# Rounded three-pass input projections in the second layer of a two-block transformer kernel

## The reference, cut to what matters

```python
hx = adaln(x, norm1_g[layer], mod_x[0], mod_x[1]); hc = adaln(ctx, ...)
qa_x, ka_x, va_x, qm_x, km_x, vm_x, om_x, gt_x = split_columns(hx @ w_in)
qa_c, ka_c, va_c, qm_c, km_c, vm_c, om_c, gt_c = split_columns(hc @ w_in)
att_x = window_attention(q, k, v, k_ctx, v_ctx, sink_g)          # 8 heads, softmax with a sink
h_xf, h_xb = mlstm_chunkwise(conv(qm), conv(km), vm, gates ...)  # forward and backward memory
out_x = merge_groups(att_x, h_xf + flip(h_xb), om_x, ...)        # @ w_out
```

## Time and profile before

| | us |
|---|---|
| median of 3 runs (lowest, highest) | 2455.31 (2447.01, 2457.3) |
| profiled execution | 2452.7 |
| its span | 2450.9 |
| TensorE busy | 2379.6 (97%) |
| DVE busy | 1808.3 (74%) |
| ACT busy | 1306.2 (53%) |
| GpSimd busy | 86.3 (4%) |

### The profile page before, as it was taken

One profiled execution on the slowest core, in us unless ns is written; L12 is line 12 of the kernel. 1 busy time (PEld: TensorE's weight loads), 2 busy tenths in 40 slices (PEclk: granted clock), 3 DMA queues, 4 the chain that ended last, 5 costly groups with the idle time before them and its releaser, 6 DMA issues.

```text
span 2450.9 us, 33383 instructions
## 1 busy us (share of the span) xinstructions
PE 2379.6 (97%) x13253; PEld 1953.4 (80%) x13253; DVE 1808.3 (74%) x2855; ACT 1306.2 (53%) x1971; POOL 86.3 (4%) x89
## 2 busy tenths in 40 slices
PE   7999899999999998999999999999999999999998
PEld 2575558788777776888888888888798999989997
DVE  6764577677553545999999999999867776677774
ACT  3245332222233444877877778777744654546554
POOL 0000010000010000000000000000000001100002
PEclk8999999999999999999999999999999999999999
DMA  7411045555432114989889889898843455434552
GB/s 296 180 61 35 1 154 192 190 204 188 151 138 86 52 35 173 361 329 356 343 329 366 332 329 367 331 367 331 314 173 121 155 181 198 166 127 145 182 190 103
DMA packets 71651, 510.68 MB, mean 208 GB/s; under 512 B 7905, under 2 KB 9057, under 8 KB 10049
## 3 DMA queue, kind: packets, MB, share of 16 engines
q1 hardware_dynamic: 68690, 500.21, 54.8%
q10 hardware_dynamic: 2208, 6.32, 0.7%
q0 software_dynamic: 592, 1.97, 0.2%
HBM read 506.23 MB, written 2.23 MB: 207 GB/s over the span
## 4 chain that ended last, share of the span: by engine, by line
PE 88%; DVE 7%; ACT 4%; issue 1%; DMA 1%; ACTq 0%; DVEq 0%
PE bank L815 86%; DVE UL L2238 2%; ACT UH L1703 1%; PE bank L1273 1%; DMA consts<-in_c 1%; PE bank L952 1%; DVE arena L2246 1%; DVE HT L2238 0%; ACT L1706 0%; DVE arena L3026 0%; ACT arena L1706 0%; DVE arena L2238 0%; ACT arena L1949 0%; DVE arena L2242 0%; DVE small L2305 0%
## 5 line engine op out<-in xcount | busy, mean ns | idle before, releaser
L2238 DVE TENSOR_TENSOR UL<-ring,UH 128x1024 fp32r<-128x1024 f32 (+1 forms) x804 | 975.1, 1220 | 313.2 <-ACT UH L1703 293.3
L1703 ACT CAST UH<-ring 128x1024 fp32r<-128x1024 f32 (+1 forms) x804 | 834.8, 1041 | 572.2 <-PE bank L815 543.0
L815 PE MATMUL bank<-XH,UH 128*128 128x256 f32 x1040 | 298.4, 288 | 11.3 <-ACT XH L1706 8.2
L815 PE MATMUL bank<-UH,HGh 128*128 128x512 f32 (+1 forms) x768 | 291.3, 379 | 3.9 <-issue 2.8
L815 PE MATMUL bank<-XH,UL 128*128 128x256 f32 x1040 | 294.1, 284 | 0.0
L815 PE MATMUL bank<-XL,UH 128*128 128x256 f32 x1040 | 288.9, 284 | 0.0
L815 PE MATMUL bank<-UH,HGl 128*128 128x512 f32 (+1 forms) x768 | 288.3, 375 | 0.0
L815 PE MATMUL bank<-UL,HGh 128*128 128x512 f32 (+1 forms) x768 | 287.4, 374 | 0.0
L2285 DVE CUSTOM_DVE_ANT_0 JUNK<-ring,CROW 128x1024 bf16<-128x1024 f32 x176 | 210.2, 1237 | 15.6 <-ACT CROW L1706 9.6
L815 PEld LDWEIGHTS bank<-XH,UH 128*128 128x128 f32 x1040 | 200.6, 193 | 14.7 <-issue 10.3
L815 PEld LDWEIGHTS bank<-XH,UL 128*128 128x128 f32 x1040 | 200.6, 193 | 0.0
(11 more groups left out here) (231 smaller groups left out, 3940.5 us busy)
## 6 DMA issues: line engine op xcount, KB each, us to landing
ring<-in_w SPq DMA_DIRECT2D x477, 1024.0 KB, 4.8
XT<-in_x ACTq DMA_DIRECT2D x2, 1024.0 KB, 11.8
bias_scratch<-BIAS POOLq DMA_DIRECT2D x6, 192.0 KB, 2.1
consts<-in_c ACTq DMA_DIRECT2D x1, 1109.0 KB, 8.1
out_y<-XT ACTq DMA_DIRECT2D x2, 512.0 KB, 3.5
BIAS<-bias_scratch POOLq DMA_DIRECT2D x1, 768.0 KB, 6.8
constd<-in_c ACTq DMA_DIRECT2D x1, 768.0 KB, 4.2
consts<-in_c ACTq DMA_DIRECT2D x1, 512.0 KB, 17.3
```

What stands on the lines that cost most here:

```text
L815: return e.matmul(out, lhsT, rhs, start=start, stop=stop, skip_group_check=True)
L1703: return e.copy(out, in_)
L2238: return e.tensor_tensor(out, a, b, op)
```

## The change

The input projections of layer 1 go over to the second way, with three float32r products.

- `conv_in` is removed. cp2 and cp3 run as a `duo` (one unit each, input blocks in the outer loop, the data's low parts two blocks late), then cp0, cp1, q0 to q3 and kf as `split` steps of one unit each.
- Values and gates are regrouped. One pass over 272 columns (attention values 128, gates 16, the memory values of head 0, 128) in three units of 3, 3 and 2 input blocks; one pass over 384 columns (heads 1 to 3) in four units of 2 blocks, 768 columns each. All four token blocks are worked on within each unit.
- om becomes eight units of 512 columns.
- The low parts of the four 384-column units and of the eight om units are made on GpSimd, one at the place of the step in its program; its `since` clear moves from the `mxz` step to `emt_mm`.
- Low parts overwrite the ring slot in place, so a slot comes free only when the products of its units are done. High parts lie in two thirds of the fourth ring slot and in a free buffer, so this stage has three ring slots. (The ring returns to four in the expert stage.)
- The data's high parts (`HHM`) are made by ACT behind each affine pass, their low parts (`HL`) by DVE over `H`.
- Three units are cast ahead of the root. In the split and value steps the look-ahead is one unit (`UNITS - 1`).
- `BESIDE[1]` becomes (1, 3, 3, 3) behind the four 384-column steps and (1, 2, 1, 2, 1, 2, 1, 2) behind om.

```diff
-          {"vm": (0, 1, 1, 1, 1, 2, 2, 2), "om": (1, 2, 1, 2, 1, 1, 1, 2)})
+          {"vm": (1, 3, 3, 3), "om": (1, 2, 1, 2, 1, 2, 1, 2)})
...
-            out.append(("conv_in", l, [((("cp", l, j), k), "w_in", (l,), [(128 * k, 768 + 128 * j, 128)])
-                                       for j in range(4) for k in range(8)]))
-            for j in range(4):
+            duo(("cp", l, 2), ("cp", l, 3), "w_in", (l,), 1024, 1152)
+            out.append(("evict", ("cp", l, 2)))
+            out.append(("evict", ("cp", l, 3)))
+            for j in range(2):
+                split("cp", l, j, key="w_in", idx=(l,), c0=768 + 128 * j)
                 out.append(("evict", ("cp", l, j)))
...
+            for ks in ((0, 1, 2), (3, 4, 5), (6, 7)):
+                name = ("vg", l, 0, ks[0])
+                out.append(("rows1", l, 0, ks, [(name, "w_in", (l,), [(128 * k, c, n) for k in ks
+                                                                      for c, n in ((640, 128), (2304, 16), (1280, 128))])]))
...
+        for j in range(4 * l):
+            ks = (2 * j, 2 * j + 1)
+            name = ("vg", l, 1, ks[0])
+            out.append(("rows1", l, 1, ks, [(name, "w_in", (l,), [(128 * k, 1408, 384) for k in ks])]))
+            if j == 0:
+                for _ in range(6):
+                    more()
+            beside("vm", j)
...
+        def by_pool(u):
+            name = W.units[u]
+            return W.stage_of[u] == "mixed" and (name[0] == "vg" and name[2] == 1 or name[0][0] == "om")
...
+            if stage == "mixed":
+                n, off, _ = W.at[piece]
+                o = W.place[n] * SLOT + off
+                return u, (YSlt[:, 512:512 + w], ring_[:, 3 * SLOT:3 * SLOT + w], ring_[:, 3 * SLOT + UNIT:3 * SLOT + UNIT + w])[i], ring_[:, o:o + w]
...
+            def mixed(st, t0):
+                tile, (piece, _, _, parts) = st[1], st[2][0]
+                k0 = piece[1]
+                b = psum(tile) if k0 else take(w, tile)
+                u, wh, wl = unit(piece)
+                w.wait_ge(*low_at(u))
+                for j in range(len(parts)):
+                    k = k0 + j
+                    c = slice(128 * j, 128 * j + 128)
+                    w.wait_ge(*vec.at("lm", k))
+                    mm(b[:, 0:512 - t0], wh[:, c], HHM[k][:, t0:512], k == 0, False)
+                    mm(b[:, 0:512 - t0], wh[:, c], HL[:, k, t0:512], False, False)
+                    i = mm(b[:, 0:512 - t0], wl[:, c], HHM[k][:, t0:512], False, k == 7)
...
+            def values_by_token(st):
+                ...
+                    for tb in range(4):
+                        t = slice(128 * tb, 128 * tb + 128)
+                        dst = psum(tiles[tb])[:, 0:n]
+                        mm(dst, HHM[k][:, t], wh[:, c], k == 0, False)
+                        mm(dst, HHM[k][:, t], wl[:, c], False, False)
+                        i = mm(dst, HL[:, k, t], wh[:, c], False, k == 7)
...
+                    split_high(unit(st[2][-1][0])[0], {"f1": UNITS + 1, "f3": UNITS + 1, "om": UNITS - 1, "q": UNITS - 1, "cp": UNITS - 1,
+                                                       "kf": UNITS - 1}.get(st[1][0], UNITS))
...
+                        split_high(W.first["mixed"], UNITS)
                         root(tile, 4)
...
+                elif kind == "rows1" and st[2] == 1 or kind == "split" and l[0] == "om":
+                    u, hi, lo = unit(st[-1][0][0])
+                    w.wait_ge(*hi_ready.at(u))
+                    e.tensor_tensor(lo, wap(W.units[u]), hi.bitcast(F32), ALU.subtract).then_inc(*pool.up(("low", u)))
```

More of the change, by code:

```diff
@@ L478, in __init__ @@
         stage, stretch = None, 0
+        self.place, self.turn, self.earlier = [], [], []
         for st in single(steps):
-            if st[0] in ("ffn", "route", "second", "ahead"):
+            if st[0] in ("ffn", "route", "second", "ahead") or st == ("mix", 1):
                 stretch += 1
                 self.first[st] = len(self.units)
+            if st == ("mix", 1):
+                stage = "mixed"
+                self.first[stage] = len(self.units)
             if st[0] in ("ffn", "route", "second"):
@@ L680, in build @@
         rb = view(BIAS, 768, 128)
+        HHM = [HHC[:, 512 * k:512 * k + 512] for k in range(6)] + [HHG[:, 512 * k:512 * k + 512] for k in range(2)]
         def staged(k):
@@ L1024, in join_part @@
                     give(tile)
[L1026 to L1040, removed]
-                give(*tiles)
             def down_part(k, m):
@@ L1713, in split_high @@
                     w.wait_ge(*loaded(W.units[u]))
+                    if stage == "mixed" and u == W.first[stage] + 1:
+                        released(w, max(n for n in range(W.at[W.units[u]][0]) if W.place[n] == RING - 1))
                     if u - W.first[stage] >= UNITS:
@@ L3143, in gpsimd_program @@
                     clear(arena[:, 14864:15888], "mxz", l)
+                elif kind == "rest" and st[2] == "emt_mm":
                     w.wait_ge(*vec.at("u", l))
@@ L3172, in sync_program @@
             for n in range(W.n):
-                if n >= RING:
-                    for kind, name in W.held[n - RING]:
-                        if kind in SPLITS:
-                            w.wait_ge(*lo_ready.at(W.unit[name]))
-                        elif kind == "pump":
-                            w.wait_ge(*vec.at(*name))
-                        elif kind == "rows":
-                            w.wait_ge(*sums.at("rows", name[1], name[2] // 4))
-                        elif kind in ("gemm", "conv_in"):
-                            w.wait_ge(*sums.at(*name[0]))
-                        else:
-                            w.wait_ge(*sums.at(*name[0], 3))
-                e.dma_start(ring[:, (n % RING) * SLOT:(n % RING + 1) * SLOT], w_in[n]).then_inc(s_ring[n % RING], 16)
+                if W.earlier[n] is not None:
+                    released(w, W.earlier[n])
+                i = W.place[n]
+                if i == RING - 1 and n > W.at[W.units[W.first["mixed"]]][0]:
+                    w.wait_ge(*sums.at("unit", W.last[W.first["mixed"]] - 1))
+                e.dma_start(ring[:, i * SLOT:(i + 1) * SLOT], w_in[n]).then_inc(s_ring[i], 16)
         def begin():
```

155 lines of the change are left out of this document (129 added, 26 removed).

## The result

The changed kernel took 2470.0 us (median of 4, 2469.11 to 2478.28), the kernel before on the same chip 2453.58 (4 runs, 2447.01 to 2457.3). The ratio is 1.0074, with a 95% interval of 1.0049 to 1.0099: slower by 16.4 us, where 12.5 were forecast (2467, range 2448 to 2484). In time, the interval of the ratio is 12.0 to 24.3 us, so it does not tell 12.5 from 16.4.

What follows compares the result with a forecast made beforehand. TensorE was taken to bound the stretch, busy all but 1.2 of 135.8 us. Its gain of 16.7 us and the added waits, pacing and clock summed to +12.5 us, giving 2467 us, range 2448 to 2484.

Steps and rivals of the forecast that it cites:

- TensorE's own work, -16.7: Layer 1's input projections: TensorE's products go from 90.5 to 73.8 us, a gain of 16.7 if nobody waits.
- Start, +1.4: Start of the stage: ACT casts three units before the root, which comes near 735.7 instead of 734.1, +1.4 us.
- the pacing by ACT, +2.6: Convolution inputs: ACT needs 1.65 us per 512-column block, TensorE 1.37; 13.6 instead of 11.0 us, +2.6.
- DVE before q2 and q3, +8.4: Convolutions in DVE's queue delay the low parts of q2 and q3; TensorE waits 3.0 and 5.4 us.
- Values and gates, +0.8 and +1.0: Head 0's values and gates: ropes' DVE operations precede a low part, +0.8 us; four gate copies lie open, +1.0.
- First low part on GpSimd, +4.5: Before the 384-column part: TensorE waits for GpSimd's clear (0.95) and 768-column subtraction (2.0), +4.5 us with hand-overs.
- Attention, +7.1: Attention beside the value and om units: casts one unit ahead come late in ACT's queue, +7.1 us, bounds 0 and 12.
- Clock, +3.4, bounds 0 to 6.8: Low clock behind the waits before q3 and the first GpSimd unit, 1.7 us less work per stretch, +3.4 us.
- Two signs that I had named: Right if memory's first transposes come at 880 to 890 us; wrong if another stage moves by over 2 us.
- slow GpSimd: Rival: GpSimd's low parts in value and om units take 4.4 and 2.9 us, not 2.0 and 1.3; +9.5, 2477; chance 0.14.
- The lock of GpSimd and DVE: Rival: GpSimd low parts and DVE's softmax operations hold each other up, 1.07 us per hit; +6.4, 2474; chance 0.08.
- weight loads set the pace: Rival: 256-column passes run at the 0.193 us weight load, not 0.119; +17.8 us on top, 2485; chance 0.04.

Runs made afterwards that it cites:

- experiment 3: Changed kernel with bf16 filler products on constants in TensorE's waits before q2, q3 and the 384-column part: 2464.47 us (1.0042).
- experiment 10: Kernel with the edits of experiment 2, Experiment 5, experiment 6 and experiment 7, but only q2's low parts on GpSimd, q3's and kf's on DVE: 2455.01 us (1.0005).
- Experiment 5: Changed kernel with ACT's root ahead of the casts (two units then, not three) and DVE's inverse ahead of its first low parts: 2465.84 us (1.0046).
- experiment 1: Changed kernel with four of five convolution taps left out in layer 1, leaving out part of the computation: 2463.78 us (1.0044).
- experiment 2: Changed kernel with the first 384-column low part on DVE, the eleven others on GpSimd: 2461.92 us (1.0038).
- experiment 6: Changed kernel with ACT casting two units ahead instead of one in the 384-column and om steps: 2465.74 us (1.0051).
- 4 against 2: Changed kernel with all twelve GpSimd low parts on DVE, 2465.46 us (1.0051), against the one with only the first moved, 2461.92 us.
- experiment 7: Changed kernel with low parts of q2, q3 and kf on GpSimd and casts two units ahead up to kf: 2466.35 us (1.0056).

## Why the prediction was right, and where it was not

The direction, its mechanism and most of its terms held. The sum was 12.5, where the medians show 16.4 (12.0 to 24.3) and one stage 17.4. By its steps:

- *TensorE's own work, -16.7.* Held. With the clock up, experiment 3 shows the attention stretch at 75.46, against 82.57 - 13.4 + 7.1 = 76.3 by the forecast's terms without the clock. TensorE's busy time there was 67.82 at a clock of 1.00 (experiment 10), against 81.90 at 0.98 before.
- *Start, +1.4, and the pacing by ACT, +2.6.* +1.9 and, with the products' -4.0, -1.5. The root came 4.57 us behind the moments instead of 3.18, +1.4 as forecast (the forecast's own times, 735.7 against 734.1, give 1.6). Experiment 5 turns the first off alone (8.34).
- *DVE before q2 and q3, +8.4.* The place and the cause are shown by the timeline of DVE and by experiment 1. The idle times were 2.72 and 2.74 instead of 3.0 and 5.4: q2 ran at the lower clock, took 5.1 instead of 2.9 and so hid part of the second wait. The stretch came out as forecast (+8.3, against +7.8), because in it a low clock and a wait share the same time: the idle times, with kf's 0.68, make 6.1 us where the forecast had 8.4 of waiting, and the clock makes the rest. I had noted that kf might start up to 3 later; experiment 1 shows that wait, covered in the changed kernel.
- *Values and gates, +0.8 and +1.0.* The stretch moved by +4.4, against +4.8.
- *First low part on GpSimd, +4.5.* +4.3 measured, and shown by experiment 2. The subtraction took 1.80 for 768 columns, against my 2.0.
- *Attention, +7.1.* Mechanism shown by experiment 6 for the part that GpSimd releases (a cast allowed one unit ahead); idle times of 0.68, 1.94, 2.05 and 0.75 beside smaller ones. The idle time of the stretch went from 0.67 to 5.66, so the term came to 5.0 and was 2.1 too large, which hid part of what the clock cost.
- *Clock, +3.4, bounds 0 to 6.8.* The least certain term, and too small for the profiled execution. I took one stretch of 3.4 us at the lower level behind each of two long waits. The changed kernel has seven such stretches, 37.4 us, four of them of 6.8. Four of them stand at or behind waits of 2.0 to 4.1 us (q2, q3, the 384-column part, 864.9). The others stand where TensorE has few products, such as those of gates and scans at 823 to 830, 14 instructions in 6.8 us; the kernel before has its second low stretch behind the same products. In attention the clock cost this execution some 9 us (busy 76.86, against 67.82 in experiment 10) and the one of experiment 1, with the same code and waits, some 3 (70.64). Experiment 3 puts the price of the stretches that the fillers remove at 5.5 us between medians and at most 9.5 between profiled executions. The upper bound assumed that every low stretch is as short as the one in the earlier trace rows and stands behind a wait of over 2 us; both fail here. That the whole came within 4 us of the forecast is in part luck: attention's waits were put too high by 2.1 and the clock too low, and how often a low stretch appears varies from execution to execution.

Two signs that I had named do not look as I wrote. The memory's first transposes came at 897.17, not at 880 to 890, and a stage outside the change moved by over 2 us: the statistics came at 735.85 instead of 730.93. But in the twelve profiled executions of the changed kernel and its variants, which run the same code up to there, the statistics came at 729.59 to 736.53, and all that lies outside the stage took 2306.8 to 2316.5 us (2307.0 before). So these 4.9 us are within the scatter of executions.

Of the rivals, slow GpSimd did not happen (1.80 us for the 768 columns, 1.27 for 512 where I feared 4.4 and 2.9). The lock of GpSimd and DVE cost the changed kernel no more than moving the low parts to DVE does (4 against 2). As a mechanism it is real and larger than the 1.07 of the earlier trace rows: 6.2 us in experiment 7, 2.15 in experiment 10. Of this the Trainium skill, page SBUF — State Buffer, section "SBUF: two separate sides", says that the later engine blocks for the whole instruction of the other; the trace agrees, with 2.15 us lost beside an operation of 2.39.

That weight loads set the pace is excluded by the starts of the 256-column products (here cp0's), 0.12 apart where a mean load takes 0.193:

```profile
759.27 0.28 PE L884 MATMUL bank<-HHC,ring_rounded 128*128 128x256 f32 x1
759.39 0.28 PE L884 MATMUL bank<-HTr,ring_rounded 128*128 128x256 f32 x1
```

What stays open: why a low stretch follows a wait in one execution and not in another, and with it how much of the 16.4 us is clock.

## What to carry to other kernels

When TensorE's work shrinks in a stage, write down for each engine what stands in its queue ahead of the next operand; a convolution of 4.7 us that nobody waited for becomes a wait as soon as a projection takes 2.9. Price the clock with the waits: removing one wait of 4.1 us took 8.1 off the median, and filling three waits without bringing any operand earlier took 5.5. Before the length of a stage in one profiled execution is put down to an edit, compare a stretch that the edit leaves alone: here the same attention stretch took 76.75, 80.11 and 82.52 us. An operand made on GpSimd should be off the path by its cast, not only by its length, and what DVE runs beside it must be work that may take longer (6.2 us longer in experiment 7).

## What the runs showed of the hardware

- Behind idle times of only 2.72 and 2.74 us TensorE ran 6.8 and 3.4 us at a granted clock near 0.5; I had expected one stretch of 3.4 for the longer waits alone. Busy with bf16 products on constants in these waits, it stayed at 1.00 (experiment 3).
- The same wait does not always bring a low stretch: behind one of 2.05 us there was one of 3.4 in three profiled executions and none in three others.
- A GpSimd subtraction to float32r takes 1.80 us for 768 columns and 2.39 for 1024, DVE's 1.22 for 1024. A group of four scalar-tensor-tensor operations on DVE took 2.15 us longer beside one of 2.39 (experiment 10).
